# Value products of two heads issued alternately in the grid attention of a two-block transformer kernel

## What is computed

```
scores = jnp.concatenate([s_loc.reshape(bsz, nh, GRID_W, n_loc), s_ctx], axis=-1)
p = jax.nn.softmax(scores.astype(jnp.float32), axis=-1).astype(v.dtype)
p_loc = p[..., :n_loc].reshape(bsz, nh, GRID_W, kh, NA_COLS)
return (jnp.einsum("bhwrk,brwkhd->bwhd", p_loc, v_win)
        + jnp.einsum("bhwc,bchd->bwhd", p[..., n_loc:], v_ctx))
```

## Time and profile before

| | |
|---|---|
| Median of the timed executions | 1022.42 us (1021.97 to 1022.79) |
| Span of the profiled execution (the page gives no other time of it) | 1021.6 us |
| TensorE (PE) busy | 990.6 us, 97% |
| VectorE (DVE) busy | 696.0 us, 68% |
| ScalarE (ACT) busy | 512.6 us, 50% |
| Records of the value products, L1233 | 64, mean 385 ns |
| Mean granted TensorE clock | 0.996 |

### The profile page before, as it was taken

The page is one execution under the profiler, slowest core; times in us unless marked ns, Lnnn a source line. Parts: engine busy times, 40 slices in busy tenths (PEclk is TensorE's granted clock), DMA queues, the critical chain, the costliest instruction groups (busy, mean ns, idle before and its releaser), DMA issues. The chain is left out here.

```text
span 1021.6 us, 15144 instructions
## 1 busy us (share of the span) xinstructions
PE 990.6 (97%) x5976; PEld 860.0 (84%) x5976; DVE 696.0 (68%) x996; ACT 512.6 (50%) x687; POOL 48.3 (5%) x61
## 2 busy tenths in 40 slices
PE   7999999999989999999999999999998989999997
PEld 5577899999978877899998988988865779999996
DVE  5776647777775665657778564456598587777775
ACT  2366474544545665545454463544445354444443
POOL 0220000000000110000001010000010000000000
PEclk9999999999999999999999999999999999999999
DMA  9035576667664533568887543234101245545541
GB/s 363 16 101 147 206 278 222 249 249 277 230 223 141 192 122 115 215 250 326 293 326 285 211 163 115 92 124 165 42 1 42 104 164 192 185 185 184 187 177 42
DMA packets 29727, 183.92 MB, mean 180 GB/s; under 512 B 3440, under 2 KB 6128, under 8 KB 10096
## 3 DMA queue, kind: packets, MB, share of 16 engines
q1 hardware_dynamic: 25360, 157.56, 43.0%
q0 software_dynamic: 3456, 25.17, 6.7%
q10 hardware_dynamic: 864, 0.55, 0.2%
HBM read 180.64 MB, written 2.62 MB: 179 GB/s over the span
## 5 line engine op out<-in xcount | busy, mean ns | idle before, releaser
L1904 DVE TENSOR_TENSOR split<-raw,split 128x2048 fp32r<-128x2048 f32 (+1 forms) x123 | 279.9, 2275 | 203.5 <-ACT split L1374 202.2
L1374 ACT ACTIVATE split<-raw 128x2048 fp32r<-128x2048 f32 x122 | 231.8, 1900 | 248.3 <-PE bank L683 219.0
L681 PE MATMUL bank<-acts,split 128*128 128x256 f32 (+1 forms) x1024 | 290.8, 284 | 2.3 <-DVE acts L1944 1.4
L683 PE MATMUL bank<-acts,split 128*128 128x256 f32 (+1 forms) x1024 | 289.7, 283 | 0.0
L682 PE MATMUL bank<-acts,split 128*128 128x256 f32 (+1 forms) x1024 | 289.6, 283 | 0.0
L681 PE MATMUL bank<-split,acts 128*128 128x512 f32 (+1 forms) x544 | 211.4, 389 | 0.6 <-DVE split L1904 0.4
L682 PE MATMUL bank<-split,acts 128*128 128x512 f32 (+1 forms) x544 | 209.3, 385 | 0.0
L683 PE MATMUL bank<-split,acts 128*128 128x512 f32 (+1 forms) x544 | 209.1, 384 | 0.0
L681 PEld LDWEIGHTS bank<-acts,split 128*128 128x128 f32 (+1 forms) x1024 | 194.7, 190 | 6.0 <-DVE split L1904 1.9
L682 PEld LDWEIGHTS bank<-acts,split 128*128 128x128 f32 (+1 forms) x1024 | 194.7, 190 | 2.5 <-issue 0.2
L683 PEld LDWEIGHTS bank<-acts,split 128*128 128x128 f32 (+1 forms) x1024 | 194.7, 190 | 0.4
(11 more groups left out here) (250 smaller groups left out, 1065.8 us busy)
## 6 DMA issues: line engine op xcount, KB each, us to landing
raw<-w_mlp SPq DMA_DIRECT2D x64, 1024.0 KB, 4.8
raw<-w_glu SPq DMA_DIRECT2D x22, 1024.0 KB, 4.8
bias<-w_ada POOLq DMA_DIRECT2D x14, 1024.0 KB, 6.8
raw<-w_qkv SPq DMA_DIRECT2D x12, 1024.0 KB, 4.7
arena<-w_glu_down SPq DMA_DIRECT2D x22, 512.0 KB, 3.3
work<-w_ada POOLq DMA_DIRECT2D x10, 1024.0 KB, 7.0
raw<-w_mla_o SPq DMA_DIRECT2D x4, 1024.0 KB, 5.8
raw<-w_moba_o SPq DMA_DIRECT2D x4, 1024.0 KB, 4.8
```

The source lines that it names most:

```text
L681: pe.matmul(out_, a[0], b[0], start=first, stop=False)
L683: return pe.matmul(out_, a[1], b[0], start=False, stop=last)
L1374: return act.activation(out_, in_, ACT.Copy)
L1904: v.tensor_tensor(split[:, c % 2, 1, 0:n], raw[:, c % 2, 0:n], split[:, c % 2, 0, 0:n].bitcast(F32), ALU.subtract).then_inc(lo_ready, 1)
```

## The change

For heads 0 to 5 the value products are issued by pair. The new kind OO p (p = 0, 1, 2) does heads 2p and 2p + 1 in one block: for each of the four key groups the product of the even head (partitions 0 to 63 of `pair_bank`) and then that of the odd head (64 to 127). OO p stands at the end of step 4p + 4, where O 2p + 1 stood; O 2p, two steps earlier, is gone from its place. O 6 and O 7 stay as they were.

The probabilities of head 2p are now read later than the P of head 2p + 2 is transposed, and both use the same slot. So ScalarE's copies of P 4, P 8 and P 12 wait for the end of OO 0, OO 1 and OO 2 (`pair_ready`).

```
--- before.py
+++ after.py
@@ -190,8 +190,10 @@
             steps.append(("S", i + 3))
         if i - 1 in DECAY:
             steps.append(("Y", DECAY.index(i - 1)))
-        if i % 2 == 0 and i:
-            steps.append(("O", i // 2 - 1))
+        if i in (4, 8, 12):
+            steps.append(("OO", i // 4 - 1))
+        if i == 2 * H - 2:
+            steps.append(("O", H - 2))
     steps.append(("O", H - 1))
...
@@ -1219,6 +1221,20 @@
+                elif kind == "OO":
+                    for n in range(4):
+                        small_gone(pe, window_unit("P", 4 * i + n))
+                    if i == 0:
+                        gemm_gone(pe, ku + 5)
+                    else:
+                        pe.wait_ge(pair_free, i)
+                    for k in range(4):
+                        for e in range(2):
+                            h = 2 * i + e
+                            val = (nv if k < 2 else ncv)[:, k % 2, h * 64:(h + 1) * 64]
+                            ins = pe.matmul(pair_bank[64 * e:64 * e + 64, 0:T], val,
+                                            view(att, 2048 + 1024 * e, 4, T)[:, k, :], start=k == 0, stop=k == 3)
+                    ins.then_inc(pair_ready, 1)
@@ -1775,6 +1791,8 @@
                     h, t = (i - 1) // 2, (i - 1) % 2
                     u = window_unit("P", i - 1)
                     small_out(act, u)
+                    if i - 1 in (4, 8, 12):
+                        act.wait_ge(pair_ready, (i - 1) // 4)
                     copy(view(att, 2048 + 1024 * (h % 2), 4, T)[:, :, t * P:(t + 1) * P], halves(u, 4, P))\
                         .then_inc(small_free[u % 4], 1)
```

## The result

The changed kernel takes 1025.37 us (median of 12 executions, 1022.86 to 1028.72), the kernel before, on the same chips, 1022.72 us (12 executions). The ratio is 1.0023, interval 1.0016 to 1.0030: about 2.4 us slower. Sent again later it gave 1024.4 us (12 executions, 1023.0 to 1029.4) beside 1022.78 us, ratio 1.0017, 1.0007 to 1.0027. Its executions are spread over 6 us where those of the kernel before lie within 2. The profiled execution took 1026.52 us, with a span of 1024.7 us, 3.1 us more than the span before.

A forecast was written before the change was run, and what follows sets the result against it. It took TensorE and VectorE, both nearly full and handing work to each other, as the bound. Lateness from the ScalarE waits, partly given back, came to +1.4 us on 1022.4: 1023.8 us, range 1022.0 to 1027.9.

The forecast's parts named there:

- the 0.2% band: Total times counted as "same": within 2.0 us, 1020.4 to 1024.5 us; chance of same 0.48.
- The likeliest case: Pair blocks overlap and lateness is given back as worked out: 1023.8 us, reaching from 1022.0 to 1025.0; chance 0.55.
- the case without overlap: Rival: the two column tiles in OO do not overlap, each block 3.60 us, +5.3 us, 1027.7 us; chance 0.26.
- O 0, O 2 and O 4 leave: On TensorE, each block's removal takes away 2.01 us there; OO 0 starts 0.64 us before O 1 did, at 753.82.
- The length of OO: Pair block on TensorE: 2.30 us taken, between 2.09 at full overlap and 2.51 with tile-change costs; entering three times.
- the sum of +1.4 us: Net change forecast against the profiled span of 1021.6 us; +0.7 us with OO at 2.09, +2.0 with 2.51.
- The wait on ScalarE: Copy of P 4 waits for OO 0, delaying exponential 6 to 756.72 and logits 7 by 1.66 us; G 5 late too.
- What is given back: VectorE's 1.17 us gap before the carried rows goes; lateness falls to 0.40 us there, 0.12 us at OO 1.
- A granted clock of 1.00, so the clock is no term here.: For the stage, read from the profile before: the clock adds no term to the sum.
- The half rate of a float32 record: Argument for the no-overlap rival: both records of a product in the pair block are half-rate float32.
- That TensorE's time counts in full: Rival: TensorE is the bound and the stage shrinks by what leaves it, -4.8 us, 1017.6 us; chance 0.10.
- That more is lost at the hand-overs: Rival: overlap, but no pair repays anything, each costing 1.66 us: +5.0 us, 1027.4 us; chance 0.09.

The follow-up runs named there:

- The filled kernel: The changed kernel with 3, 3 and 2 matmuls of unread result put into TensorE's gaps before P 6, P 12 and P 14: 1023.24 us, ratio 1.0004.
- The kernel with the wait alone: The kernel before with only ScalarE's three waits added (copies of P 4, P 8, P 12 wait for O 1, O 3, O 5): 1027.84 us, ratio 1.0043.
- the third slot: The changed kernel with probabilities of heads 2 and 6 in finished bias-table columns and ScalarE's three waits removed: 1020.18 us, ratio 0.9980.
- The third slot, head by head: The third slot with the even head's products all ahead of the odd head's in each pair block: 1022.16 us, ratio 0.9994.

## Why the prediction was right or wrong

The time of 1025.37 us lies in the range of 1022.0 to 1027.9, 1.6 us above the forecast of 1023.8; it is outside the 0.2% band by 0.9 us in the first measurement and inside it (1024.4) in the second. That it lies in the range is in part luck. The likeliest case, the one that came true, reached only to 1025.0; the range went up to 1027.9 for the case without overlap, which didn't happen. And two terms were wrong, in opposite directions.

- *O 0, O 2 and O 4 leave.* Right. OO 0 starts at 753.72 in a trace that began this stage 0.10 us earlier, so at 753.82 as worked out.
- *The length of OO.* The term was mis-sized: I took 2.30 us, between 2.09 and 2.51, and it measures 1.88. Even my lower end was too high, because I let each tile's records run abreast only from the second one on. Both tiles start at once, loads included: two loads and two matmuls at 753.72. Entering three times, that is -1.26 us on the sum of +1.4 us: +0.1 us is what the argument should have given for the work alone. The filled kernel shows about 0.5 us. Most of the rest lies behind OO 2, where normalise 14 starts 3.84 us after the block's start (789.07 to 792.91) and the terms of the sum give 3.49 us with the true length: the copy of P 12 begins 0.39 us after the block's last end (791.02 to 791.41), against 0.11 us for the copy of P 4. Why is not shown.
- *The wait on ScalarE.* Right in place and mechanism: exponential 6, decay 3, mask matrix 3, logits 7, G 5. Logits 7 are 1.20 us late in the trace, 1.30 us with the earlier start of the stage; the sum gives 1.66 - 0.42 = 1.24 us with the block's true length. The kernel with the wait alone shows it by itself.
- *What is given back.* Right: in the filled kernel, counted from S 3, OO 1 starts 0.14 us and OO 2 0.32 us ahead of the old places of O 3 and O 5. In the changed kernel's profile OO 1 is 0.71 us late, beyond the 0.5 us that I named; that is the first fall.
- *"A granted clock of 1.00, so the clock is no term here."* This step failed. It was read from the kernel before, where no gap in this stage is over 1 us. The change moves waiting onto TensorE: 1.69 and 0.65 us around P 6, 1.50 us before P 12. I had worked out that G 5 would start late and that "TensorE waits there", and did not ask what the clock does after such a wait. The two falls of the profile cost 2.4 to 2.7 us for which the sum has no term, and their number and length differ from one execution to the next. The trace of the kernel before had the sign too, outside the stage: 0.74 after the gap of 1.70 us at 305.84.

Of the rivals, no overlap falls by the trace: the weight loads of the second column tile start together with those of the first (two at 753.72, two at 753.99; in the third slot, where the names tell the heads apart, at 768.36 and 768.37), in the same 128 rows, and the 16 records take 1.95 us. The half rate of a float32 record, which I put down for this rival, is in the trace of the kernel before: records of 256 float32 columns start 0.217 us apart, and records of 512 columns over the split operands 0.23 us (794.04, 794.27, 794.50). It did not keep the two tiles apart. That TensorE's time counts in full does not hold, even without the waits: six O blocks less three OO take 12.1 - 3 x (1.88 + 0.14) = 6.0 us off it, and the third slot gains 2.6 us. That more is lost at the hand-overs holds for the 0.4 us above at most; what else was lost on top was clock.

## What to carry to other kernels

Two float32 matrix products that fill 64 columns each cost TensorE here no more than one (1.88 against 1.87 us), if they are issued alternately to the two column halves, and 2.79 us if one head's products all stand ahead of the other's; look for such pairs wherever heads are small. Moving a product later to form the pair keeps its operands alive longer, so give them a buffer of their own: the wait that protects a shared one stood on ScalarE ahead of the next exponential, which started 2.2 us later, and cost more than the overlap brought (5.0 us alone, 1.6 to 2.6 us with the pair blocks). Where a change moves waiting onto TensorE, add to its price what the clock loses after the gap (here two falls to 0.50, 2.4 to 2.7 us in the profile), and compare executions by their granted clock before explaining a difference (1028.6 us at 0.990 and 0.991, 1023.3 us at 0.997 and above, with one program). What the lost clock cost in time was less here than TensorE's own loss of 3.0 us, since part of that would have been waiting anyway.

## What the runs showed of the hardware that was not expected

- Two column tiles of 64 ran fully abreast in float32 with 128 rows and 256 columns each: 16 records in 1.95 us, 8 in 1.94 us.
- TensorE started matmuls of the other column tile out of the order of its list: with all of one head first, the ninth record starts 0.01 us after the fifth and ahead of the sixth, seventh and eighth. The third slot, head by head, shows it with the heads told apart (770.22 us ahead of 770.43).
- A gap of 1.69 us with one of 0.65 us shortly behind it, and one of 1.50 us, were each followed by 3.4 us at 0.50 of the clock in the profile of the changed kernel (worked out from the stretches of one microsecond, 761 to 766 and 785 to 789), a gap of 1.69 us with one of 0.54 us by 6.8 us in that of its repetition (760 to 767). A fall took TensorE 1.5 us in the first and 2.9 us in the second (5.99 against 3.10 us from G 5 to F 2). Which gaps have a fall behind them differs between executions of one program: after the gap of 1.50 us the clock is 0.50 in the first profile and 1.00 in the second. With matmuls whose result nobody reads put into the gaps, the stage has no fall in the profile (1.00), and none of 11 executions has a mean clock under 0.996.
